# Gate and up products of four feed-forward stages as 2x2 block products with seven products for eight

## The reference

```python
def rmsnorm_2(x, g):
    xf = x.astype(jnp.float32)
    y = xf * lax.rsqrt(jnp.mean(xf * xf, axis=-1, keepdims=True) + EPS)
    return (y * g.astype(jnp.float32)).astype(x.dtype)

def swiglu(h, w_gu, w_down):
    g, u = jnp.split(h @ w_gu, 2, axis=-1)
    return (jax.nn.silu(g) * u) @ w_down
...
        x = x + 0.5 * swiglu(rmsnorm_2(x, ffn1_norm[l]), ffn1_w_gu[l], ffn1_w_down[l])
```

## Time and profile before

| | us |
|---|---|
| median of 3 runs | 2967.66 |
| lowest and highest | 2964.74, 2968.47 |
| profiled execution | 2963.42 |
| its span | 2961.6 |

### The profile page before, as it was taken

One profiled execution on the slowest core, in us unless ns is written; L12 is line 12 of the kernel. 1 busy time (PEld: TensorE's weight loads), 2 busy tenths in 40 slices (PEclk: granted clock), 3 DMA queues, 4 the chain that ended last, 5 costly groups with the idle time before them and its releaser, 6 DMA issues.

```text
span 2961.6 us, 33736 instructions
## 1 busy us (share of the span) xinstructions
PE 2837.4 (96%) x13230; PEld 2308.0 (78%) x13230; DVE 1569.1 (53%) x2381; ACT 1106.9 (37%) x1722; POOL 240.4 (8%) x255
## 2 busy tenths in 40 slices
PE   6997998999999999999899999999999998999999
PEld 5776776888878888887678888888887776788887
DVE  6467664555555444446854444544444876543443
ACT  4444553322224222343733222422223775432322
POOL 1000222000000000001300000000000542100000
PEclk9999998999999999999899999999999998899999
DMA  3212203333323323232023233333321010123332
GB/s 130 74 55 73 60 31 92 105 101 99 93 82 104 100 93 100 86 100 72 15 78 99 94 100 93 95 99 98 100 84 65 31 43 22 50 93 100 94 98 79
DMA packets 71182, 242.60 MB, mean 82 GB/s; under 512 B 8016, under 2 KB 9936, under 8 KB 70768
## 3 DMA queue, kind: packets, MB, share of 16 engines
q1 hardware_dynamic: 68112, 230.85, 25.1%
q0 software_dynamic: 1760, 7.49, 0.7%
q10 hardware_dynamic: 1152, 2.10, 0.2%
HBM read 238.31 MB, written 2.10 MB: 81 GB/s over the span
## 4 chain that ended last, share of the span: by engine, by line
PE 89%; DVE 5%; ACT 3%; issue 1%; POOL 1%; DMA 0%; DVEq 0%; POOLq 0%; ACTq 0%
PE ps L301 88%; PE ps L304 1%; DVE SC L324 1%; ACT SC L309 1%; DVE SC L312 1%; DVE SM L330 1%; POOL SC L312 1%; DVE WL L312 0%; POOL SC L319 0%; ACT WH L309 0%; ACT L309 0%; DMA PR<-par 0%; DVE PTL L312 0%; DVE SC L327 0%; ACT PTH L309 0%
## 5 line engine op out<-in xcount | busy, mean ns | idle before, releaser
L301 PE MATMUL ps<-HH,WH 128*128 128x512 f32 (+1 forms) x2192 | 864.5, 394 | 14.7 <-DVE HL L324 13.8
L301 PE MATMUL ps<-HL,WH 128*128 128x512 f32 (+1 forms) x2192 | 856.6, 391 | 0.0
L301 PE MATMUL ps<-HH,WL 128*128 128x512 f32 (+1 forms) x2192 | 856.5, 391 | 0.0
L312 DVE TENSOR_TENSOR WL<-WF,WH 128x1024 fp32r<-128x1024 f32 (+3 forms) x473 | 545.6, 1158 | 371.6 <-ACT WH L309 368.1
L309 ACT ACTIVATE WH<-WF 128x1024 fp32r<-128x1024 f32 (+3 forms) x473 | 467.3, 993 | 641.0 <-PE ps L301 640.9
L301 PEld LDWEIGHTS ps<-HH,WH 128*128 128x128 f32 (+1 forms) x2192 | 413.5, 189 | 103.8 <-issue 16.1
L301 PEld LDWEIGHTS ps<-HH,WL 128*128 128x128 f32 (+1 forms) x2192 | 412.8, 188 | 87.8
L301 PEld LDWEIGHTS ps<-HL,WH 128*128 128x128 f32 (+1 forms) x2192 | 413.4, 189 | 84.3 <-issue 0.2
L301 PE MATMUL ps<-AH,WH 128*128 128x512 f32 x880 | 343.4, 390 | 3.9 <-DVE AL L312 3.9
L301 PE MATMUL ps<-AL,WH 128*128 128x512 f32 x880 | 343.0, 390 | 0.0
L301 PE MATMUL ps<-AH,WL 128*128 128x512 f32 x880 | 342.9, 390 | 0.0
(11 more groups left out here) (288 smaller groups left out, 2968.4 us busy)
## 6 DMA issues: line engine op xcount, KB each, us to landing
WF<-wall SPq DMA_DIRECT2D x397, 512.0 KB, 3.5
WF<-wall SPq DMA_DIRECT2D x40, 384.0 KB, 3.0
WF<-wall SPq DMA_DIRECT2D x17, 256.0 KB, 2.6
X<-xT ACTq DMA_DIRECT2D x8, 256.0 KB, 12.3
X<-xT POOLq DMA_DIRECT2D x8, 256.0 KB, 3.0
outT<-X POOLq DMA_DIRECT2D x8, 256.0 KB, 2.3
WF<-wall SPq DMA_DIRECT2D x4, 288.0 KB, 2.9
LT<-late POOLq DMA_DIRECT2D x1, 1152.0 KB, 5.6
```

The lines of the kernel that those rows point to most:

```text
L301: return self.real.matmul(o, l, r, start=start, stop=stop, skip_group_check=True)
L312: return self.real.tensor_tensor(o, a, b, op) if self.real is not None else Uncounted()
```

## The change

In the stages 2, 4, 5 and 7 (FAST) the units from 5 on (LEAD) are computed otherwise. The weights of a unit form a matrix of 2 x 2 blocks: gate or up by the first or last 512 of the 1024 features. The tokens form one too: the same two halves of the features by the first or last 256 tokens. The product of two such matrices needs seven block products and a number of sums (the scheme of Winograd). The new kernel makes on the tokens, once a stage, the sums `t0` to `t3` (with gain and norm factor already on them) and their halves B1, B2, TP and TQ; and on the weights, for each unit, four sums. Of these one comes from a plain load with an adding DMA of GpSimd (`fe`, second half), one likewise (`fh`), one is made by GpSimd (`sum2`, first half of `fe`) and one by VectorE (`sum4`, second half of `fz`). The products are `a11`, `a12`, `s1`, `s2`, `s3`, `a22`, `s4`, each 4 blocks of 3 matmuls with 256 columns; several add up in one PSUM bank with copies taken out between them (`e1`, `e2`, `e3`), the rest of the sums are made by VectorE (`c11`, `c22`, `c21`, `c12`).

The order of the work in such a stage now comes from a table of times (`F_PLACE`, `work_f`), for all engines. The pieces per unit are `fa`, `fe`, `fz` of 1024 and `fh` of 512 numbers a partition, with `fh` and `fz` of one unit used beside `fa` and `fe` of the next. NWF goes from 4 to 7, the activation slots NA from 10 to 8, the descriptor space of software DMAs is set to 4096. The first unit's up product is cut in two, with the sums of the norm ahead of it and their spreading between its halves. LP is loaded after the last product of stage 2 instead of after the first out-projection.

```diff
-NWF = 4
+NWF = 7
+FAST = (2, 4, 5, 7)
+LEAD = 5
...
+    for c, (m0, n) in enumerate(CHUNKS):
+        units = range(max(m0, LEAD), m0 + n)
+        for m in units:
+            last = m == units[-1]
+            t3, t22, t4 = (now + 7, now + 10, now + 11) if last else (now + 9, now + 12, now + 13)
+            at(now + F_PLACE["added"], "w_add", m)
+            at(now + F_PLACE["sum2"], "w_sum2", m)
+            at(now + F_PLACE["sum4"], "w_sum4", m)
+            at(now, "a11", m)
+            spent(now + 1, "a12", m)
+            at(now + 3, "s2", m)
+            spent(now + 4, "s1", m)
+            spent(t3, "s3", m)
+            at(t22, "a22", m)
+            spent(t4, "s4", m)
...
+            now += 7
...
+        def weights_left(n):
+            p = n - NWF
...
+            left = [w_low[p]]
...
+                if name == "fa":
+                    left.append(pooled[f"F{s}", "sum2", m])
+                    if of_unit[p][3]["fz"] != n:
+                        left.append(stepped[f"F{s}", "sum4", m])
+                elif name == "fe":
+                    left.append(stepped[f"F{s}", "sum4", m])
...
         def sync_program(e):
...
+            for n, (name, _, _, r, c) in enumerate(plan):
+                for w in weights_left(n):
+                    e.wait_ge(*w)
...
+                if name == "fe":
+                    done = e.dma_start(buf[:, 512:1024], in_wall(n, 512, 1024))
+                elif name in ("fh", "fz"):
+                    of = of_unit[n][3]["fe"]
+                    done = e.dma_start(buf[:, 0:512], in_wall(of, 0, 512) if name == "fh" else in_wall(of, 512, 1024))
...
+            def form(s, stage, m, ph, kind, moving, first):
+                n, p = fast_piece(s, stage, m), bank(ph, kind, m)[:, 0:256]
+                half = 0 if stage in ("a11", "s2", "s3", "a22") else 4
+                wh, wl = wview(WH, n, NWS), wview(WL, n, NWS)
...
+                e.wait_ge(*w_low[n])
+                tokens, a = moving
+                for k in range(4):
+                    e.wait_ge(*split_low[ph, "t", k])
+                    r = tuple(t[:, k, a:a + 256] for t in tokens)
+                    for i, (l, rr) in enumerate(three((wh[:, half + k, :], wl[:, half + k, :]), r)):
+                        done = e.matmul(p, l, rr, first and k == 0 and i == 0, k == 3 and i == 2)
...
+                    elif stage == "a11":
+                        form(s, stage, key, ph, "sa", (B1, 0), True)
+                    elif stage == "a12":
+                        form(s, stage, key, ph, "sb", (B2, 0), True)
+                    elif stage == "s2":
+                        e.wait_ge(*copied[ph, "e1", key])
+                        form(s, stage, key, ph, "sa", (TQ, 0), False)
+                    elif stage == "s1":
+                        form(s, stage, key, ph, "sc", (TP, 0), True)
+                    elif stage == "s3":
+                        e.wait_ge(*copied[ph, "e2", key])
+                        form(s, stage, key, ph, "sa", (TP, 256), False)
+                    elif stage == "a22":
+                        e.wait_ge(*copied[ph, "e3", key])
+                        form(s, stage, key, ph, "sa", (TQ, 256), False)
+                    elif stage == "s4":
+                        e.wait_ge(*stepped[ph, "c22", key])
+                        form(s, stage, key, ph, "sc", (B2, 256), False)
...
+                    elif stage == "w_add":
+                        at = of_unit[fast_piece(s, "s2", key)][3]
+                        for name, a in (("fe", 512), ("fh", 0)):
+                            n = at[name]
+                            e.wait_ge(s_slot[n % NWF], 16 * (n // NWF + 1))
+                            e.dma_add(WF[:, n % NWF, a:a + 512], in_wall(at["fe" if name == "fe" else "fa"], 0, 512))\
+                             .then_inc(s_added[n % NWF], 16)
+                    elif stage == "w_sum2":
...
+                        e.wait_ge(s_slot[fa % NWF], 16 * (fa // NWF + 1))
+                        e.wait_ge(s_added[fe % NWF], summed_up[fe])
...
+                        e.tensor_tensor(WF[:, fe % NWF, 0:512], WF[:, fe % NWF, 512:1024], WF[:, fa % NWF, 0:512], ALU.add)\
+                         .then_inc(*pooled(ph, "sum2", key))
...
+                        e.wait_ge(*pooled[ph, "sum2", key])
+                        e.tensor_tensor(WF[:, fz % NWF, 512:1024], WF[:, fe % NWF, 0:512], WF[:, fa % NWF, 512:1024], ALU.add)\
+                         .then_inc(*stepped(ph, "sum4", key))
...
-            e.wait_ge(*projected[piece["wo"][7]])
+            fast_ffn(2)
+            e.wait_ge(*projected[fast_piece(2, "s4", FM - 1)])
             e.dma_start(LP[:, :], latep).then_inc(s_late, 16)
```

More of the change, by code:

```diff
@@ L513, in ffn @@
         ph, out = f"F{s}", []
+        if s in FAST:
+            for stage, key in work_f():
+                out.append((ph, stage, key))
+                if stage == "rms_sums":
+                    out += rms(s)
+                if stage == "d_add" and key[0] == 2 and then is not None:
+                    m = key[1]
+                    out += [("X", "tile", (then, m))] + sums(then, [m - 1] if m else [])
+            return out
         for c, (m0, n) in enumerate(CHUNKS):
@@ L592, in ps_takes @@
         return [(ph, "a", key), (ph, "b", key)]
+    if ph[0] == "F" and int(ph[1:]) in FAST:
+        if stage in FAST_PS:
+            return [(ph, FAST_PS[stage], key)]
+        if stage in ("up_b0", "up_b"):
+            return [(ph, "b", key)] if (stage == "up_b0") == (key == 0) else []
+        if stage == "down":
+            return [(ph, "out", key[1]) if key[0] == 2 else (ph, "down", key[:2])] if key[2] == 0 else []
+        return []
     if stage == "merged":
@@ L616, in ps_drops @@
         return [(ph, "a", key), (ph, "b", key)]
+    if ph[0] == "F" and int(ph[1:]) in FAST:
+        if stage in FAST_PS_LEFT:
+            return [(ph, FAST_PS_LEFT[stage], key)]
+        if stage == "d_add":
+            return [(ph, "out", key[1]) if key[0] == 2 else (ph, "down", key)]
+        return []
     if stage == "merged":
@@ L637, in sc_takes @@
         return [(ph, "g", key), (ph, "v", key)] + ([(ph, "fpad", key)] if ph == "F1" else [])
+    if ph[0] == "F" and int(ph[1:]) in FAST:
+        return [(ph, kind, key) for kind in FAST_SC.get(stage, ())]
     if stage == "merged":
@@ L653, in sc_drops @@
         return ([(ph, "fpad", key)] if ph == "F1" else []) + [(ph, "v", key), (ph, "g", key)]
+    if ph[0] == "F" and int(ph[1:]) in FAST:
+        return [(ph, kind, key) for kind in FAST_SC_LEFT.get(stage, ())]
     if stage == "merged":
@@ L812, in build @@
         s_slot = [sem(f"s_w{i}") for i in range(NWF)]
+        s_added = [sem(f"s_added{i}") for i in range(NWF)]
         signals = []
@@ L1025, in build @@
                 last, split_after[n] = n, []
-                upto = next(i for i in itertools.count() if i not in done) + AHEAD
+                upto = next(i for i in itertools.count() if i not in done) + (3 if n in within else AHEAD)
             else:
```

467 lines of the change are left out of this document (420 added, 47 removed).

## The result

The changed kernel takes 2941.4 us in the median (2933.4 to 2944.0) against 2967.3 for the kernel before in the same series: a ratio of 0.991 (95% interval 0.989 to 0.993). It is 26 us faster. The forecast was 57.9 us faster: the sign and the place of the gain were right, the size was not half of what was forecast. The profiled execution took 2942.0 us, with a span of 2939.6.

The account below looks back on a forecast made before the run. TensorE, busy 96% of the span, was taken as the bound. -70.2 - 4.2 + 10.2 + 4.8 + 1.5 = -57.9 us off the median 2967.7 gave 2909.8 us, with 0.55 for 2898 to 2924 and a range of 2890 to 2950.

Parts of the forecast that it names:

- The gain on TensorE: Units 5 to 21 of four feed-forward stages: 84 matmuls of 256 columns replace 48 of 512, 70.2 us saved.
- At 0.1197: 56: Gain on the 68 changed units, 56 us, if a 256-column matmul takes 0.1197 us instead of the chosen 0.1173.
- The third rival: Fast units: 128-column weight loads no longer hide, so half the columns is not half the time; about 2980 us, chance 0.04.
- passed-on holds: Fast units: GpSimd's sum holds back VectorE steps; 0.15 us a unit reaches TensorE, 10.2 us lost in all.
- the chunks' starts: First unit of each of 12 runs of fast units has less time per piece; 0.4 us each, 4.8 us lost.
- the ring: Slot of `fh`: load, adding DMA, GpSimd's sum into `fe`, split, next load; 6.7 us for a period of 9.85.
- The second rival: Slot of `fh`: load, add and sum in series set the period, at 11.6 us a unit; 3013 us, chance 0.11.
- The boundary: Start of each of four feed-forward stages: 12 matmuls fill TensorE's 1.06 us wait for the norm; 4.2 us gained.
- the loads at the start: Kernel start: seven load slots issue 1.5 MB more beside the parameter load; 0 to 3.5 us lost, 1.5 taken.
- the signs named ahead for a wrong forecast: Fast units: `fh` late, GpSimd waiting and TensorE idle; a pitch above 0.12; waits over 0.5 us in most units.
- the outer range: Whole kernel: from full hiding (2890 us) to a stall of 0.75 us a unit (2950 us).
- half hidden: Fast units: GpSimd's holds and the fixed order pass 0.5 us a unit to TensorE, 34 us; 2934 us, chance 0.18.

Follow-up runs that it names:

- The experiment on widths: Kernel before, gate and up products of units 5 to 21 with other stationary and moving widths in four stages; stages 2, 4, 5, 7 took 373.07, 362.21, 366.56, 320.6 us.
- all three edits: Changed kernel with GpSimd's sum before the adding DMA of `fh`, splits behind down pieces moved, and `a22` before a chunk's first down piece; 2925.2 us, ratio 0.986.

## Why the prediction was right or wrong

By the terms of the sum, for the four stages (the forecast: -70.2 - 4.2 + 15.0 = -59.4; measured -27.9).

*The gain on TensorE: the mechanism was right, and the step that failed is the price of a 256-column matmul.* Of the two prices that lay before me, 0.1173 by the earlier trace rows and 0.1197 taken down from the earlier trace rows, I took the one with the right number of columns and the wrong stationary tile, and gave as a reason that a 128-column weight load hides under the 288-column matmul. That does not answer whether the fixed part is the same. The experiment on widths says it is not: 0.1200. A unit costs 84 x 0.120 = 10.08 us, not 9.85; the gain is 0.80 x 68 = 54.4 us, 15.8 less than forecast (of which 0.2 is a slip: 68 x 1.03 is 70.0, not 70.2). "At 0.1197: 56" stood in the text as a bound and was right to 2 us. The third rival needed 0.1295, and was not the case. The rule of the Trainium skill (TensorE: Matmul & The Clock Gate, "Wait — 56ns, not 53.3ns?"), with 2.5 ns above columns / 2.4 GHz, would have put the gain at 81 us; the measured surplus is 13.3 ns at 128 columns of stationary tile (0.1200 - 0.1067), and the measurement decides.

*The waits: the total was off by 5.9 us, and the places were wrong.* Forecast were 10.2 us of passed-on holds and 4.8 at the chunks' starts; measured are 20.9. That the totals lie so near is luck: the holds came to nothing, and 15.8 us stand where the sum had no term.
- The step "0.15 a unit for holds" fell: the holds are there (1203 ns for 686), and cost nothing with the ring cut. The reason given for a small number, the spare time, holds for zero.
- "At each of the 12 runs of fast units the first unit has only four products before the next" named the starts of the chunks. There and in the units behind them 5.0 us are lost, by the ring, close to the 4.8 but by another mechanism.
- The ends of the chunks, the second step that failed, were left out altogether: 10.8 us at first down pieces and 5.0 at third ones. I had counted the free time of the slots from one unit into the next, and not into the down piece, where one product of 1.44 us covers two splits of 2.3. That the slot order changed there too was to be read in the list.

*The second rival was right in its place and wrong in its size.* It asked whether the ring sets the period and found 6.7 us by the rows. (It would set it from 9.85 us on; 10.9 is where nothing would be gained.) One pass of it in stage 4 took 8.8. A ring below the period was counted as harmless. It was not: 136 issues at 0.97 us instead of 0.56, landings of 3.0 and 4.3 instead of 2.6, and above all a queue in order, in which `sum2` stood behind a wait for `fh`. What the ring cost in the stages is 7 to 10 us: 1418.2 and 1420.7 in two executions of the changed kernel, 1411.0 to 1411.3 in the three kernels without it.

*The boundary* went as forecast: three of the four waits for the norm are gone, the fourth is 0.81 us where each was 1.10 as an idle gap; together 3.6 us for the forecast 4.2.

*What is left.* -54.4 - 3.6 + 20.9 makes -37.1, and measured is -27.9. Of the other 9.2 us, 7.8 are what the 30 waits cost beyond their length, 0.26 us each, as shown above; the sum of the prediction had no term for it. With the ring cut the same sum is -54.4 - 3.6 + 15.6 = -42.4 for a measured -37.6 (1411.0 less 1448.6). There 16 waits are left, and the starts of the matmuls give 4.2 of the 4.8 us. The remainders, 1.4 and 0.6 us, are small single steps. So the 31.5 us by which the stages missed the forecast are 15.8 for the price of a matmul, 7.8 for what the waits cost beyond their length, 5.9 for their length, 0.6 at the boundary and 1.4 of small steps.

*Elsewhere.* I allowed 1.5 us for the loads at the start. That term is neither shown nor excluded: stage 2 starts at 918.0 and 918.4 in the two profiled executions with four slots and at 918.7 to 924.5 in the eleven with seven (919.9 in that of the changed kernel), and the median with the slots alone is 0.8 us above that of before. (By 11.81 us, 3.8 MB had landed, not some 5.) What made the changed kernel's profiled execution longer is in the stretch between the stages 5 and 7, which the change doesn't touch: the stretch of before, of after, and of the kernel with two splits moved (columns as in the earlier trace rows):

```profile
2255.89:2593.95 338.06, 300.63 (x1520) 234.12 (x1518) 221.30 (x408) 201.66 (x386) 109.19 (x107) 0.93 0.12 37
```
```profile
2236.85:2580.97 344.12, 306.03 (x1520) 237.24 (x1518) 221.61 (x409) 201.66 (x386) 110.29 (x107) 0.92 0.12 40
```
```profile
2222.81:2569.22 346.41, 306.75 (x1520) 238.06 (x1519) 222.96 (x411) 202.73 (x388) 110.45 (x107) 0.91 0.12 40
```

The work is the same (x1520 matmuls), TensorE is busy with it for 300.6, 306.0 and 306.8 us, and the granted clock is 0.93, 0.92 and 0.91: in more of its time TensorE is at 1.2 GHz. The same kernel, run again, took 339.0 there. The time outside the four stages lies between 1511.9 and 1522.2 us in the profiled executions of the changed kernel and its variants, with 1513.0 for before and 1515.7 for the one with slots alone. So 5 us of a difference of two single executions can be the clock, and which of it an edit brings about is open. Three of the four kernels with moved splits took 345 to 349.5 us in this stretch, the fourth 340.8; but the experiment on widths, with none of the new code and no moved split, took 344.3, so a long stretch does not need them.

*What came as said.* A steady piece of fast units, 1665 to 1735 us in stage 4: VectorE 54.9 of 70 us (78%; forecast 80%), ScalarE 56% (64%), 182 GB/s (182). The DMA share was forecast between 0.60 and 0.77; it is 0.71. The DMA queues there, packets, MB and share of 16 engines:

```profile
q1 hardware_dynamic: 3940, 9.66, 42.4%
q0 software_dynamic: 1654, 2.99, 28.4%
```

The adding DMAs (q0) take 9.5% of the engines for a MB, the plain loads (q1) 4.4%. Part of q1's packets are larger, but at the same size (2048 bytes) it is the same: 214 ns a packet in the mean with the addition, 107 without. The Trainium skill (Collectives: The Full Stack, "The bandwidth ceiling: the fold count and why AG ≠ RS ≠ AR") says of the addition in a reducing collective that it needs two source reads; the factor of two agrees. The price was hidden, as forecast. The token sums stayed hidden, nothing in the trace of after waits for LP, and the slots cost nothing measurable. Of the signs named ahead for a wrong forecast, GpSimd waiting for `fh` with TensorE idle behind it came; the pitch stands at the 0.12 that was named, waits of over 0.5 us in most units did not come, and stage 4 took 356.2 us where 343 to 348 had been named for a right one.

*The range.* The time lies outside the band that had the chance 0.55 (2898 to 2924) and inside the outer range (2890 to 2950), near the rival "half hidden" (2934); but that one had its 34 us from holds, and the time came from 15.8 us of matmul length, from waits at other places and from 7.8 us that the waits cost beyond their length. That it lies there is chance.

## What to carry to other kernels

Where a change halves the columns of a matmul, take its price from a long run of matmuls with the same stationary tile, even at another column count: here the part above the columns was the same at four column counts and differed between tiles, and the change has it 84 times a unit instead of 48. In a ring of load, add, sum and split, look at what stands behind each wait on an in-order queue, not only at the length of the ring: here one block of lines moved behind the sum was worth 14 us of 2937 in the medians (7 seen in the stages of the profiled executions), half as much as the whole change had gained. Count a slot's free time at the ends of a loop as well as in its steady part, where the step that comes next is of another kind. And price a wait of TensorE at more than its length: 0.26 us more for the short ones here, and behind those of 3.3 and 5.3 us some 2 us more, because the granted clock was lower for 4.6 to 9 us after them.

With the sum ahead of the second adding DMA and the first down piece one product later (`e9_down_later`), the kernel takes 2921.7 us: 1.5% under the kernel before, and 0.5 to 0.6% under the changed one (ratios to the kernel before: 0.9852, and 0.9909 and 0.9902 for the changed one).

## What the runs showed of the hardware that was not expected

- In long runs on the weights the distance of two matmuls of 256 columns goes with the width of the stationary tile: 0.1200 us at 128 columns, 0.1160 at 96, 0.1134 at 64. At 128 the surplus above columns / 2.4 GHz is the same for 256, 288, 384 and 512 columns: 13.3, 13.1, 13.3 and 13.3 ns. Why the width matters is not shown, and width alone is not all: the 62-column tile of the earlier trace rows has 0.1173, more than the 64 and the 96 here, and in the attention of the kernel before pairs of 256 columns with a 128-column tile (`PT,VV`) start 0.116 to 0.118 us apart at the full clock.
- A wait of TensorE costs more than the idle time that the profile shows: 0.16 us until the next start and 0.1 in the distance behind it, in all 7.8 us for 30 waits. Behind the waits of up to 1.7 us in the changed kernel the granted clock stayed at 1.00; after one of 3.32 in stage 5 it was 0.52 for 7 us with the splits moved (0.51 for 9 with all three edits), behind one of 5.34 it was 0.51 for 4.6 us.
- An adding DMA takes about twice the DMA engines' time of a plain one (214 against 107 ns for a packet of 2048 bytes) and its issue holds GpSimd for 0.97 us in the mean.
- VectorE's 512-wide low half beside GpSimd's sum took 1203 ns in the mean for 686; GpSimd's sum itself took 1587 where 1298 stood before.
- The stretch between the stages 5 and 7 took 338.1 to 349.5 us in the profiled executions, with the same work; the granted clock there is 0.92 or 0.93 in those up to 340.8 us and 0.91 or 0.92 in those from 344.1.
